# Key norms in an attention stage: from column sums, a root and spread products to products with ones, a logarithm and an exponential

## The chip, the cores and the metric

One core of one Trainium2 chip runs the whole program. The metric is the device time of one execution in microseconds (us), as the median of the runs; lower is better. TensorE multiplies matrices, VectorE, ScalarE and GpSimd work on elements, and each takes its instructions in the order in which they are written, with semaphores between them.

## The reference

The program is eight blocks on an activation x of 512 positions by 1024 channels: four mixers (a, b, c, a) and four sandwiched layers (e, f0, o, f1). Stage b is one of them, dilated window attention, with 8 heads of 128 channels and three patterns, each with its own query, key and value:

```python
def rms_norm(x, g):
    xf = x.astype(jnp.float32)
    y = xf * lax.rsqrt(jnp.mean(xf * xf, axis=-1, keepdims=True) + EPS)
    return (y * g.astype(jnp.float32)).astype(x.dtype)
...
    for g, (window, dilation) in enumerate(B_PATTERNS):
        q = apply_partial_rotary(rms_norm(qkv[:, :, 0, g], q_gain[g]), cos, sin)
        k = apply_partial_rotary(rms_norm(qkv[:, :, 1, g], k_gain[g]), cos, sin)
        o, lse = dilated_window_attention(q, k, qkv[:, :, 2, g], window // dilation, dilation)
        outs.append(o)
        lses.append(lse)
    wgt = jax.nn.softmax(jnp.stack(lses), axis=0)
    o = jnp.einsum('gbsh,gbshd->bshd', wgt, jnp.stack(outs))
    y = o.reshape(bsz, S, B_WIDTH).astype(h.dtype) * jax.nn.silu(z)
    return y @ w_out
```

Each query and each key row is divided by the root of its mean square over 128 channels. That division is what changes here.

## The kernel before

Weights come as units of 128x1024 by DMA into `raw`. ScalarE rounds a unit to the type that TensorE takes in one pass (`split_high`, L277, `w_high`), VectorE subtracts to get the rest (`split_low`, L284, `w_low`), three units ahead of TensorE. A product of a unit is 24 matmuls (`product`, L297 to L299): high by high, high by low, low by high.

Stage b works in two halves of four heads. A half begins with the values of its heads (L779 to L781), kept in `b_v`. Then comes a list of slots (j, u), written out for each engine in the same order, and `b_steps` says what a slot holds. Slot (j, u) projects tile u of head j: u = 0, 1, 2 are the keys of the three patterns, 3, 4, 5 the queries. The tile lies with channels in the partitions and the 512 positions in the row. One slot later the tile is squared, summed and turned by rotary. In slots 1 to 4 of head j the softmax of one block of 128 queries of head j-1 is done; in slots 2 to 5 the block of the slot before is transposed; in 3, 4, 5 and the next 0 it is multiplied by the values. Four slots with j = 4 project the gate z and finish the last head.

In a slot, TensorE does: the product of the tile; four column sums of the last tile's squares against a column of ones (L839, 128x1 each); value products (L853); transposes (L859 to L862); the score products, one of 128x512 (L871) and two small (L875); and in slots 4, 5 and the next 0 the spread: 1/rms of a key tile is made into a 128x512 bank by four products with the unit matrix (L885), for VectorE to multiply the keys with (L1068). The two small score products wait for ScalarE's copy of the last two transposes (L929), since they share a bank.

ScalarE in a slot: L277 for a unit ahead; the square of the new tile out of the bank (L909, in two buffers by turns); the tile with its gain (L915, "gained"); in two slots of a head a root of 12 columns (L923); copies of the transposes (L929, L931); Exp of the softmax (L934). A table load stands ahead of the root or Exp when the function set changes.

VectorE in a slot: L284; rotary on 32 rows (L1008, L1010, L1011, L1014); mean square plus epsilon (L1019) and reciprocals (L1028, L1031) in two slots of a head; scores with their scale and mask into `b_p` (L1048), maximum (L1052), its negative (L1054); behind Exp the reciprocal and the scaling of the row (L1060, L1062); the key multiply (L1068). GpSimd does nothing in stage b but the sums of squares for the next norm at its end (L325).

Of the kernel before, what the change touches and what calls it, by code (L numbers as in the profile page):

```python
# [27 lines left out]
F32 = mybir.dt.float32  # L28
# [3 lines left out]
P = 128  # L32
# [125 lines left out]
def build(nc, stream, x_in, params_in, const_in, tables_in, ssm_in, x_out):  # L158
# [10 lines left out]
    with ctx:  # L169
# [65 lines left out]
        b_root_done, b_rk_done, b_rq_done = sem("b_root_done"), sem("b_rk_done"), sem("b_rq_done")  # L235
        b_spread, b_k_done = sem("b_spread"), sem("b_k_done")
# [475 lines left out]
        b_sq = (sq, ssq)  # L712
        b_tanh = ssq[:]
# [3 lines left out]
        b_root, b_rk, b_rq = b_col[:, 0:24], b_col[:, 24:36], b_col[:, 36:60]  # L717
# [4 lines left out]
        def b_tile(j, n):  # L722
            return b_qk[:, (j % 2) * (B_TILES - 1) + n if n < B_TILES - 1 else 2 * B_TILES - 2]

# [34 lines left out]
        def b_tensor(pe, t, first, o, y_base, r, last=False, following=None):  # L759
# [39 lines left out]
            for i in range(2):  # L799
# [6 lines left out]
                for j, u in B_SLOTS:  # L806
                    unit = b_unit(first, i, j, u)
                    tile, s, tr, pv, kn = b_steps(j, u)
                    if unit is not None:
                        n = B_TILES * j + u  # L810
                        if n < 2:
                            pe.wait_ge(b_v_copied, lin(9 + n, i, 12))
                        elif j < BH or u < 2:
                            pe.wait_ge(b_gained, lin(n - 1, i, 24))
                        elif u == 2:
                            pe.wait_ge(b_args, lin(2 * BH, i, 2 * BH))
                        else:
                            pe.wait_ge(b_k_done, lin(3 * BH, i, 3 * BH))
                        product(pe, unit, ps[:, u if j == BH else n % 2], h_high, h_low)
                    elif i == 0:  # L820
                        values(1, 0, B_TAIL.index((j, u)))
                    else:
                        for k in (2 * B_TAIL.index((j, u)), 2 * B_TAIL.index((j, u)) + 1):
                            for m in range(4):
                                out_tile(m, k)
                    if (i, j, u) == (0, 0, 0):
                        norm_spread(pe, R_PRE["b"], 7).then_inc(b_r_spread, 1)
                    if tile is not None:
# [3 lines left out]
                        if tile[1] == 0 and n > 0:  # L832
                            pe.wait_ge(b_root_done, lin(2 * tile[0], i, 2 * BH))
                        if tile[1] == 3:
                            pe.wait_ge(b_root_done, lin(2 * tile[0] + 1, i, 2 * BH))
# [42 lines left out]
                    if kn is not None:  # L878
                        j0, g = kn
                        if 3 * j0 + g > 0:  # L880
                            pe.wait_ge(b_k_done, lin(3 * j0 + g, i, 12))
                        pe.wait_ge(b_rk_done, lin(j0 + 1, i, BH))
# [10 lines left out]
        def b_scalar(act, first, o, y_base, r, last=False, following=None):  # L893
            norm_root(act, R_PRE["b"])
            for i in range(2):
                for n in range(len(B_TAIL) * i, 4 * B_PATTERNS):
                    split_high(act, Unit(first + n + AHEAD, i, B_HALF))
                for j, u in B_SLOTS:
# [21 lines left out]
                    if tile is not None and tile[1] in (2, 5):  # L920
                        c = 12 * (tile[1] // 3)
                        act.wait_ge(b_args, lin(2 * tile[0] + tile[1] // 3 + 1, i, 2 * BH))
                        nc.scalar.activation(b_root[:, c:c + 12], b_root[:, c:c + 12], ACT.Sqrt).then_inc(b_root_done, 1)  # L923
# [8 lines left out]
                    if s is not None:  # L932
                        act.wait_ge(b_soft, b_soft_at(i, s[0], s[1], 5))
                        nc.scalar.activation(b_p, b_p, ACT.Exp, bias=b_neg, accum_out=b_sum).then_inc(b_exp, 1)  # L934
                    if j == BH and u < BH:
                        act.wait_ge(b_z_taken, BH * i + u + 1)
                        if u == 0:
                            act.wait_ge(b_ss, 6 * BH * (i + 1))
                        else:
# [7 lines left out]
            for m in range(KD):  # L947
# [4 lines left out]
                high_of(act, following, m)  # L952

        def b_vector(dve, first, o, y_base, r, last=False, following=None):
# [5 lines left out]
            for i in range(2):  # L960
# [25 lines left out]
                def take_z(m):  # L986
                    if i == 0:
                        dve.wait_ge(b_r_kept, 1)
                    if m == 0:
                        dve.wait_ge(b_ss, lin(6 * BH - 1, i, 6 * BH))  # L990
# [3 lines left out]
                for j, u in B_SLOTS:  # L994
# [21 lines left out]
                    if tile is not None and tile[1] in (2, 5):  # L1016
                        c = 12 * (tile[1] // 3)
                        dve.wait_ge(b_ss, lin(6 * tile[0] + tile[1] + 1, i, 24))
                        nc.vector.scalar_tensor_tensor(  # L1019
                            out=b_root[:, c:c + 12].rearrange("p (g b) -> p g b", b=NBLK),  # L1020
                            in0=ps[:, 2, c:c + 12].rearrange("p (g b) -> p g b", b=NBLK), scalar=1.0 / P,
                            in1=norm_eps.unsqueeze(1).to_broadcast([P, B_PATTERNS, NBLK]), op0=ALU.mult,
                            op1=ALU.add).then_inc(b_args, 1)
                    if tile is not None and tile[1] == 2:
                        dve.wait_ge(b_root_done, lin(2 * tile[0] + 1, i, 2 * BH))
                        if tile[0] > 0:
                            dve.wait_ge(b_spread, lin(3 * tile[0], i, 12))
                        nc.vector.reciprocal(b_rk, b_root[:, 0:12]).then_inc(b_rk_done, 1)  # L1028
                    if tile is not None and tile[1] == 5:
                        dve.wait_ge(b_root_done, lin(2 * tile[0] + 2, i, 2 * BH))  # L1030
                        nc.vector.reciprocal(b_rq[:, 12:24], b_root[:, 12:24]).then_inc(b_rq_done, 1)  # L1031
                        dve.wait_ge(b_rq_done, lin(2 * tile[0] + 1, i, 2 * BH))
                        if tile[0] > 0:
                            dve.wait_ge(b_soft, b_soft_at(i, tile[0] - 1, 3, 3))
                        nc.vector.tensor_scalar(b_rq[:, 0:12], b_rq[:, 12:24], P ** -0.5, None,
                                                op0=ALU.mult).then_inc(b_rq_done, 1)
                    if s is not None:
# [3 lines left out]
                        dve.wait_ge(b_rq_done, lin(2 * j0 + 2, i, 2 * BH))  # L1041
# [21 lines left out]
                    if kn is not None:  # L1063
                        j0, g = kn
                        n = 3 * j0 + g
                        dve.wait_ge(b_spread, lin(n + 1, i, 12))
                        dve.wait_ge(b_qk_done, lin(6 * j0 + g + 1, i, 24))
                        nc.vector.tensor_tensor(b_tile(j0, g), b_tile(j0, g), ps[:, 3], ALU.mult).then_inc(b_k_done, 1)  # L1068
# [1938 lines left out]
        def _(pool):  # L3007
            norm_gather(pool, 0)
            for n, name in enumerate(names):
                last = n == len(names) - 1  # L3010
                r = R_POST.get(name, None if last else R_PRE[name] + 1)
                if name == "e":
# [245 lines left out]
```

## Time and profile before

| | us |
|---|---|
| median of 3 runs | 3021.32 (3019.75 to 3021.74) |
| profiled execution, own time | 3030.46 |
| its span | 3028.7 |
| TensorE busy in it | 2924.4 (97%) |
| VectorE busy | 1714.8 (57%) |
| ScalarE busy | 1061.6 (35%) |
| GpSimd busy | 213.1 (7%) |

Busy times are sums over the span; matmuls are pipelined, so the duration of one is longer than the distance from its start to the next one's start. Where the text adds up time on an engine, it uses distances between starts. The slots of stage b lie between 463 and 1036 us of the span.

### The profile page before, as it was taken

What the parts mean: (1) busy time and instruction counts of PE and PEld (TensorE: products, weight loads), DVE (VectorE), ACT (ScalarE), POOL (GpSimd) and SP (SyncE); (2) the same over time, 40 slices, a digit from 0 to 9 for tenths busy, and PEclk for the clock granted to TensorE, in tenths of its full rate; (3) what the DMA queues carried; (4) which work ended last, traced back from release to release, by engine and by line L of the source; (5) the groups of instructions that cost most, each with busy time, mean ns of one, the idle gap of its engine ahead of it and who ended that gap; (6) DMA issues with size and microseconds to landing.
All of it is one profiled execution on the core that took longest, in us unless ns stands there. A gap on an engine that the chain in (4) does not pass through costs nothing.

```text
span 3028.7 us, 38678 instructions
## 1 busy us (share of the span) xinstructions
PE 2924.4 (97%) x14206; PEld 2413.4 (80%) x14206; DVE 1714.8 (57%) x2639; ACT 1061.6 (35%) x1601; POOL 213.1 (7%) x256
## 2 busy tenths in 40 slices
PE   7999999999999999999999999989999988999998
PEld 6888888888888778878888876588888875788887
DVE  5555535765576666654455576646444576464445
ACT  4332323443344332224332323434232345442222
POOL 1000000000000000001000000015502110110001
PEclk9999999999999999999999999989999999999999
DMA  4322232122221233332232331013333310223332
GB/s 146 97 96 85 92 104 77 56 63 77 78 62 56 63 105 95 95 97 90 90 97 83 97 102 45 29 55 106 92 95 96 99 63 16 62 85 96 96 97 90
DMA packets 70400, 252.14 MB, mean 83 GB/s; under 512 B 7808, under 2 KB 9856, under 8 KB 69632
## 3 DMA queue, kind: packets, MB, share of 16 engines
q1 hardware_dynamic: 68112, 241.89, 25.9%
q10 hardware_dynamic: 2016, 7.96, 0.7%
q8 instruction: 87, 1.43, 0.2%
q0 software_dynamic: 144, 0.52, 0.0%
q14 instruction: 41, 0.34, 0.0%
HBM read 248.25 MB, written 2.10 MB: 83 GB/s over the span
## 4 chain that ended last, share of the span: by engine, by line
PE 84%; DVE 8%; ACT 4%; issue 3%; POOL 1%; DMA 0%; DVEq 0%; ACTq 0%; POOLq 0%
PE ps L297 17%; PE ps L299 17%; PE ps L298 17%; PE ps L568 2%; PE ps L569 2%; PE ps L570 2%; ACT w_high L277 2%; DVE w_low L284 2%; PE ps L779 1%; PE ps L780 1%; PE ps L781 1%; PE ps L1803 1%; PE ps L853 1%; PE ps L591 1%; PE ps L839 1%
## 5 line engine op out<-in xcount | busy, mean ns | idle before, releaser
L284 DVE TENSOR_TENSOR w_low<-raw,w_high 128x1024 fp32r<-128x1024 f32 x456 | 565.8, 1246 | 420.8 <-ACT w_high L277 413.7
L297 PE MATMUL ps<-h_high,w_high 128*128 128x512 f32 x1872 | 737.8, 394 | 6.4 <-DVE arena L1464 3.0
L299 PE MATMUL ps<-h_high,w_low 128*128 128x512 f32 x1872 | 729.9, 390 | 0.0
L298 PE MATMUL ps<-h_low,w_high 128*128 128x512 f32 x1872 | 729.4, 390 | 0.0
L277 ACT ACTIVATE w_high<-raw 128x1024 fp32r<-128x1024 f32 x456 | 477.9, 1051 | 450.9 <-PE ps L299 204.0
L297 PEld LDWEIGHTS ps<-h_high,w_high 128*128 128x128 f32 x1872 | 352.3, 188 | 78.3 <-DVE arena L1464 3.4
L299 PEld LDWEIGHTS ps<-h_high,w_low 128*128 128x128 f32 x1872 | 351.8, 188 | 73.9
L298 PEld LDWEIGHTS ps<-h_low,w_high 128*128 128x128 f32 x1872 | 352.3, 188 | 70.1
L297 PE MATMUL ps<-y_high,w_high 128*128 128x512 f32 x640 | 250.4, 391 | 0.6 <-DVE y_low L1938 0.3
L298 PE MATMUL ps<-y_low,w_high 128*128 128x512 f32 x640 | 249.1, 389 | 0.0
L299 PE MATMUL ps<-y_high,w_low 128*128 128x512 f32 x640 | 249.0, 389 | 0.0
L325 POOL TENSOR_TENSOR root<-root,ssq 128x512 f32<-128x512 f32 x24 | 32.9, 1372 | 1691.5 <-ACT ssq L313 1690.0
L297 PEld LDWEIGHTS ps<-y_high,w_high 128*128 128x128 f32 x640 | 120.1, 188 | 28.0 <-DVE y_low L686 2.0
L299 PEld LDWEIGHTS ps<-y_high,w_low 128*128 128x128 f32 x640 | 120.1, 188 | 25.0
L298 PEld LDWEIGHTS ps<-y_low,w_high 128*128 128x128 f32 x640 | 120.2, 188 | 24.5
L568 PE MATMUL ps<-w_high,h_high 128*128 128x512 f32 x256 | 102.6, 401 | 11.4 <-DVE w_low L284 11.4
L569 PE MATMUL ps<-w_low,h_high 128*128 128x512 f32 x256 | 101.8, 397 | 0.0
L570 PE MATMUL ps<-w_high,h_low 128*128 128x512 f32 x256 | 101.6, 397 | 0.0
L1556 ACT ACTIVATE y_high<-full 128x512 f32 (+1 forms) x44 | 27.8, 632 | 192.2 <-DVE full L1590 192.2
L779 PE MATMUL ps<-w_high,h_high 128*128 128x512 f32 x192 | 76.8, 400 | 3.2 <-DVE x L520 2.1
L780 PE MATMUL ps<-w_low,h_high 128*128 128x512 f32 x192 | 75.8, 395 | 0.0
L781 PE MATMUL ps<-w_high,h_low 128*128 128x512 f32 x192 | 75.7, 394 | 0.0
(443 smaller groups left out, 4526.0 us busy)
## 6 DMA issues: line engine op xcount, KB each, us to landing
raw<-stream SPq DMA_DIRECT2D x456, 512.0 KB, 3.6
table<-tables_in ACTq DMA_DIRECT2D x5, 1088.0 KB, 6.5
x<-x_in ACTq DMA_DIRECT2D x8, 256.0 KB, 8.3
x_out<-x SPq DMA_DIRECT2D x16, 128.0 KB, 1.7
const<-const_in SPq DMA_DIRECT2D x1, 673.0 KB, 7.9
arena<-ssm_in POOLq DMA_DIRECT2D x1, 512.0 KB, 5.8
params<-params_in ACTq DMA_DIRECT2D x1, 287.0 KB, 6.7
```

The costliest lines, as they stand in the source:

```text
L277: nc.scalar.activation(w_high[:, u.slot], raw[:, u.raw], ACT.Copy).then_inc(weights_high, 1)
L284: nc.vector.tensor_tensor(w_low[:, u.slot], raw[:, u.raw], w_high[:, u.slot].bitcast(F32), ALU.subtract).then_inc(weights_low, 1)
L297: nc.tensor.matmul(bank, wh, high[:, k], start=k == 0, stop=False)
L298: nc.tensor.matmul(bank, wh, low[:, k], start=False, stop=False)
L299: mm = nc.tensor.matmul(bank, wl, high[:, k], start=False, stop=k == tiles - 1)
L325: nc.gpsimd.tensor_tensor(root[:], root[:], (sq, ssq)[m % 2][:], ALU.add).then_inc(norm_gathered, 1)
L568: nc.tensor.matmul(bank, hh, wh, start=k == 0, stop=False)
L569: nc.tensor.matmul(bank, hh, wl, start=False, stop=False)
L570: mm = nc.tensor.matmul(bank, hl, wh, start=False, stop=k == KD - 1)
L779: nc.tensor.matmul(bank, hh, wh, start=k == 0, stop=False)
L780: nc.tensor.matmul(bank, hh, wl, start=False, stop=False)
L781: mm = nc.tensor.matmul(bank, hl, wh, start=False, stop=k == KD - 1)
```

## The change

Only stage b changes, and in it the norms. The keys: ScalarE squares a key tile twice, once as it is and once rounded to the one-pass type (`b_halves(n)[0]`, in free rows of `y_high`); GpSimd subtracts to get the rest (new function `b_gpsimd`, into `y_low`); TensorE multiplies both parts with a 128x128 matrix of ones, which sums over the channels and leaves the sum in all 128 partitions. VectorE scales it and adds epsilon, which was spread by TensorE once at the start (`b_eps`). In slot 3, behind the softmax's Exp, ScalarE takes the logarithm of the three key tiles and then exp of minus one half of it. The key multiply reads that from SBUF. The spread products are gone. The queries keep their column sums; their 1/rms is now exp of minus half the logarithm too, for 12 columns in slot 0 of the next head. There is one buffer of squares in place of two.

```diff
-                        pe.wait_ge(b_gained, lin(n + 1, i, 24))
-                        for b in range(NBLK):
-                            c = 4 * tile[1] + b
-                            mm = nc.tensor.matmul(ps[:, 2, c:c + 1], b_blk(b_sq[n % 2], b), ones[:, 0:1],
-                                                  start=True, stop=True)
+                        if tile[1] < 3:
...
+                            pe.wait_ge(b_low, lin(3 * tile[0] + tile[1] + 1, i, 3 * BH))
+                            sq_high, sq_low = b_halves(n)
+                            nc.tensor.matmul(ps[:, 3], b_ones, sq_high, start=True, stop=False)
+                            mm = nc.tensor.matmul(ps[:, 3], b_ones, sq_low, start=False, stop=True)
...
-                    if kn is not None:
...
-                        for b in range(NBLK):
-                            col = b_rk[:, 4 * g + b:4 * g + b + 1].to_broadcast([P, P])
-                            mm = nc.tensor.matmul(b_blk(ps[:, 3], b), col, ident, start=True, stop=True)
-                        mm.then_inc(b_spread, 1)
...
-                            if n >= 2:
-                                act.wait_ge(b_ss, lin(n - 1, i, 24))
-                            nc.scalar.activation(b_sq[n % 2][:], ps[:, n % 2], ACT.Square)
+                            if n >= 1:
+                                act.wait_ge(b_ss, lin(n, i, 24))
+                            nc.scalar.activation(b_sq, ps[:, n % 2], ACT.Square)
+                            if u < 3:
+                                nc.scalar.activation(b_halves(n)[0], ps[:, n % 2], ACT.Square)
...
-                        nc.scalar.activation(b_root[:, c:c + 12], b_root[:, c:c + 12], ACT.Sqrt).then_inc(b_root_done, 1)
+                    if tile is not None and tile[1] == 5:
+                        act.wait_ge(b_args, lin(4 * tile[0] + 4, i, 4 * BH))
+                        nc.scalar.activation(b_root, b_root, ACT.Ln, scale=float(P)).then_inc(b_logs_done, 1)
...
+                        nc.scalar.activation(b_rq, b_root, ACT.Exp, scale=-0.5).then_inc(b_rq_done, 1)
...
+                    if tile is not None and tile[1] == 2:
+                        act.wait_ge(b_args, lin(4 * tile[0] + 3, i, 4 * BH))
+                        for g in range(B_PATTERNS):
+                            mm = nc.scalar.activation(b_log[g], b_log[g], ACT.Ln)
+                        mm.then_inc(b_logs_done, 1)
+                        act.wait_ge(b_logs_done, lin(2 * tile[0] + 1, i, 2 * BH))
+                        for g in range(B_PATTERNS):
+                            nc.scalar.activation(b_log[g], b_log[g], ACT.Exp, scale=-0.5).then_inc(b_rk_done, 1)
...
+        def b_gpsimd(pool):
+
+            for i in range(2):
+                for j in range(BH):
+                    for g in range(B_PATTERNS):
+                        n = B_TILES * j + g
+                        sq_high, sq_low = b_halves(n)
+                        pool.wait_ge(b_gained, lin(n + 1, i, 24))
+                        nc.gpsimd.tensor_tensor(sq_low, b_sq, sq_high.bitcast(F32), ALU.subtract).then_inc(b_low, 1)
...
+                        nc.vector.scalar_tensor_tensor(out=b_log[tile[1]], in0=ps[:, 3], scalar=1.0 / P, in1=b_eps,
+                                                       op0=ALU.mult, op1=ALU.add).then_inc(b_args, 1)
...
-                        nc.vector.tensor_tensor(b_tile(j0, g), b_tile(j0, g), ps[:, 3], ALU.mult).then_inc(b_k_done, 1)
+                        nc.vector.tensor_tensor(b_tile(j0, g), b_tile(j0, g), b_log[g], ALU.mult).then_inc(b_k_done, 1)
```

The line numbers shift by the change: square L909 to L918 (the second one L920), gained L915 to L926, copies L929 and L931 to L946 and L948, Exp L934 to L951, Ln L955 and Exp L959 for keys, L936 and L940 for queries.

ScalarE in slot 3 of a head, before. It begins with the weight rounding of the slot and ends with that of slot 4.

```order
L277 ACTIVATE w_high<-raw 128x1024
L909 ACTIVATE ssq<-ps 128x512
L915 ACTIVATE arena<-ps,params 128x512
L923 ACT_TABLE_LOAD
L923 ACTIVATE arena<-arena 128x12
L929 ACTIVATE work<-ps 128x256
L931 ACTIVATE work<-ps 128x512
L934 ACT_TABLE_LOAD
L934 ACTIVATE arena<-arena 128x768
L277 ACTIVATE w_high<-raw 128x1024
```

The same place after, from the copies of the transposes on; `full` and `const` hold the three tiles of logarithms.

```order
L946 ACTIVATE work<-ps 128x256
L948 ACTIVATE work<-ps 128x512
L951 ACTIVATE arena<-arena 128x768
L955 ACT_TABLE_LOAD
L955 ACTIVATE full<-full 128x512 x2
L955 ACTIVATE const<-const 128x512
L959 ACT_TABLE_LOAD
L959 ACTIVATE full<-full 128x512 x2
L959 ACTIVATE const<-const 128x512
L277 ACTIVATE w_high<-raw 128x1024
```

The root ahead of the copies has gone, and two table loads and six activations of 128x512 stand between the softmax's Exp and the next rounding.

ScalarE in slot 0 of the next head after the change, where the queries' 12 columns are done.

```order
L277 ACTIVATE w_high<-raw 128x1024
L918 ACTIVATE sq<-ps 128x512
L920 ACTIVATE y_high<-ps 128x512
L926 ACTIVATE arena<-ps,params 128x512
L936 ACT_TABLE_LOAD
L936 ACTIVATE arena<-arena 128x12
L940 ACT_TABLE_LOAD
L940 ACTIVATE arena<-arena 128x12
L277 ACTIVATE w_high<-raw 128x1024
```

Before, one table load and one root stood where the four rows L936 to L940 stand now, and the square was one.

TensorE in slot 2 of a head, behind the product, before and then after.

```order
L839 MATMUL ps<-const,ssq 128x1 x4
L859 MATMUL ps<-const,arena 128x128
L860 MATMUL ps<-const,arena 128x128
L862 MATMUL ps<-const,arena 128x128 x4
L871 MATMUL ps<-arena 128x512
L875 MATMUL ps<-arena 128x128 x2
```

```order
L849 MATMUL ps<-y_high 128x512
L850 MATMUL ps<-y_low,y_high 128x512
L877 MATMUL ps<-const,arena 128x128
L878 MATMUL ps<-const,arena 128x128
L880 MATMUL ps<-const,arena 128x128 x4
L889 MATMUL ps<-arena 128x512
L893 MATMUL ps<-arena 128x128 x2
```

Four products of one column have become two of 512; the rest stands as it stood.

## Rows read from the trace of the kernel before

**Rows 1.** Busy time, share and instructions, from the page.

```profile
PE 2924.4 (97%) x14206; PEld 2413.4 (80%) x14206; DVE 1714.8 (57%) x2639; ACT 1061.6 (35%) x1601; POOL 213.1 (7%) x256
```

**Rows 2.** Waits from 440 to 1110 us: who for whom, us in total, times, longest.

```profile
PEld ps L875 <- ACT work L929: 11.4, 24, 1.3
```

**Rows 3.** Groups on TensorE, 440 to 1110 us: busy us, mean ns.

```profile
L885 PE MATMUL ps<-const,arena 128*128 128x128 f32 x192 | 25.8, 278 | 0.0
```

**Rows 4.** Timeline of ScalarE: start us, duration us, slot 0 of heads 1 to 3.

```profile
508.47 0.60 ACT L909 ACTIVATE sq<-ps 128x512 f32<-128x512 f32 x1 [5.13 <-PE ps L299]
...
561.48 0.60 ACT L909 ACTIVATE sq<-ps 128x512 f32<-128x512 f32 x1 [4.84 <-PE ps L299]
...
615.84 0.60 ACT L909 ACTIVATE sq<-ps 128x512 f32<-128x512 f32 x1 [4.84 <-PE ps L299]
```

**Rows 5.** Timeline of TensorE's weight loads, slots 4 and 5 of head 2.

```profile
595.59 1.09 PEld L839 LDWEIGHTS ps<-const,ssq 128*128 128x128 f32 x8
596.61 1.42 PEld L853 LDWEIGHTS ps<-work,arena 128*128 128x128 f32 x12
...
599.14 0.19 PEld L875 LDWEIGHTS ps<-arena 128*128 128x128 f32 x1 [0.24 <-ACT work L929]
...
599.91 0.97 PEld L885 LDWEIGHTS ps<-const,arena 128*128 128x128 f32 x8
600.80 0.19 PEld L297 LDWEIGHTS ps<-h_high,w_high 128*128 128x128 f32 x1
...
606.14 1.09 PEld L839 LDWEIGHTS ps<-const,sq 128*128 128x128 f32 x8
...
609.15 0.97 PEld L885 LDWEIGHTS ps<-const,arena 128*128 128x128 f32 x8
```

**Rows 6.** Timeline of VectorE, slots 2 to 5 of head 2.

```profile
576.86 1.23 DVE L284 TENSOR_TENSOR w_low<-raw,w_high 128x1024 fp32r<-128x1024 f32 x1 [0.23 <-ACT w_high L277]
...
578.76 0.68 DVE L1010 TENSOR_TENSOR root<-root,table 32x512 f32<-32x512 f32 x1
...
580.68 1.25 DVE L1048 SCALAR_TENSOR_TENSOR arena<-ps,arena,table 128x512 f32<-128x512 f32 x3
...
585.25 1.23 DVE L284 TENSOR_TENSOR w_low<-raw,w_high 128x1024 fp32r<-128x1024 f32 x1 [0.23 <-ACT w_high L277]
...
604.49 0.68 DVE L1068 TENSOR_TENSOR arena<-arena,ps 128x512 f32<-128x512 f32 x1
605.09 1.22 DVE L284 TENSOR_TENSOR w_low<-raw,w_high 128x1024 fp32r<-128x1024 f32 x1
```

**Rows 7.** ScalarE: timeline of head 2, then its group for Tanh.

```profile
562.68 1.28 ACT L923 ACT_TABLE_LOAD   x1
563.97 0.21 ACT L923 ACTIVATE arena<-arena 128x12 f32<-128x12 f32 x1
...
583.14 0.94 ACT L934 ACTIVATE arena<-arena 128x768 f32<-128x768 f32 x1 [3.31 <-DVE arena L1054]
...
584.08 1.05 ACT L277 ACTIVATE w_high<-raw 128x1024 fp32r<-128x1024 f32 x1
...
606.57 0.60 ACT L909 ACTIVATE ssq<-ps 128x512 f32<-128x512 f32 x1 [1.89 <-PE ps L299]
607.06 0.68 ACT L915 ACTIVATE arena<-ps,params 128x512 f32<-128x512 f32 x1
609.08 0.38 ACT L929 ACTIVATE work<-ps 128x256 f32<-128x256 f32 x1 [1.34 <-PE ps L860]
...
L941 ACT ACTIVATE ssq<-sq 128x512 f32<-128x512 f32 x4 | 2.5, 633 | 5.6 <-DVE sq L992 5.1 <-DVE root L972 0.5
```

**Rows 8.** GpSimd and VectorE at the end of stage b, timelines.

```profile
1043.22 1.29 POOL L325 TENSOR_TENSOR root<-root,ssq 128x512 f32<-128x512 f32 x1 [657.11 <-ACT ssq L313]
1047.70 2.52 POOL L325 TENSOR_TENSOR root<-root,sq 128x512 f32<-128x512 f32 x1 [3.19 <-ACT sq L313]
...
1043.35 2.25 DVE L284 TENSOR_TENSOR w_low<-raw,w_high 128x1024 fp32r<-128x1024 f32 x1
```

More of the change, by code:

```diff
@@ L827, in b_tensor @@
                         norm_spread(pe, R_PRE["b"], 7).then_inc(b_r_spread, 1)
+                        pe.wait_ge(b_v_copied, 12)
+                        for b in range(NBLK):
+                            mm = nc.tensor.matmul(b_blk(ps[:, 3], b), norm_eps[:, b:b + 1].to_broadcast([P, P]), ident,
+                                                  start=True, stop=True)
+                        mm.then_inc(b_r_spread, 1)
                     if tile is not None:
@@ L831, in b_tensor @@
                             pe.wait_ge(b_v_copied, lin(12, i, 12))
[L832 to L835, printed above, removed]
-                        pe.wait_ge(b_gained, lin(n + 1, i, 24))
-                        for b in range(NBLK):
-                            c = 4 * tile[1] + b
-                            mm = nc.tensor.matmul(ps[:, 2, c:c + 1], b_blk(b_sq[n % 2], b), ones[:, 0:1],
-                                                  start=True, stop=True)
+                            if i == 0:
+                                pe.wait_ge(b_r_kept, 2)
+                        if tile[1] < 3:
+                            if tile[1] > 0:
+                                pe.wait_ge(b_args, lin(4 * tile[0] + tile[1], i, 4 * BH))
+                            elif n > 0:
+                                pe.wait_ge(b_args, lin(4 * tile[0] - 1, i, 4 * BH))
+                            pe.wait_ge(b_low, lin(3 * tile[0] + tile[1] + 1, i, 3 * BH))
+                            sq_high, sq_low = b_halves(n)
+                            nc.tensor.matmul(ps[:, 3], b_ones, sq_high, start=True, stop=False)
+                            mm = nc.tensor.matmul(ps[:, 3], b_ones, sq_low, start=False, stop=True)
+                        else:
+                            if tile[1] == 3 and n > 3:
+                                pe.wait_ge(b_args, lin(4 * tile[0], i, 4 * BH))
+                            pe.wait_ge(b_gained, lin(n + 1, i, 24))
+                            for b in range(NBLK):
+                                c = 4 * tile[1] + b
+                                mm = nc.tensor.matmul(ps[:, 2, c:c + 1], b_blk(b_sq, b), ones[:, 0:1],
+                                                      start=True, stop=True)
                         mm.then_inc(b_ss, 1)
@@ L1015, in b_vector @@
                                                 ALU.add).then_inc(b_qk_done, 1)
-                    if tile is not None and tile[1] in (2, 5):
-                        c = 12 * (tile[1] // 3)
+                    if tile is not None and tile[1] < 3:
+                        if (i, tile) == (0, (0, 0)):
+                            dve.wait_ge(b_r_kept, 2)
                         dve.wait_ge(b_ss, lin(6 * tile[0] + tile[1] + 1, i, 24))
+                        nc.vector.scalar_tensor_tensor(out=b_log[tile[1]], in0=ps[:, 3], scalar=1.0 / P, in1=b_eps,
+                                                       op0=ALU.mult, op1=ALU.add).then_inc(b_args, 1)
@@ L1019, in b_vector @@
+                    if tile is not None and tile[1] == 5:
+                        dve.wait_ge(b_ss, lin(6 * tile[0] + 6, i, 24))
                         nc.vector.scalar_tensor_tensor(
-                            out=b_root[:, c:c + 12].rearrange("p (g b) -> p g b", b=NBLK),
-                            in0=ps[:, 2, c:c + 12].rearrange("p (g b) -> p g b", b=NBLK), scalar=1.0 / P,
+                            out=b_root.rearrange("p (g b) -> p g b", b=NBLK),
+                            in0=ps[:, 2, 12:24].rearrange("p (g b) -> p g b", b=NBLK), scalar=1.0 / P,
@@ L1029, in b_vector @@
[L1029 to L1036, printed above, removed]
```

47 lines of the change are left out of this document (21 added, 26 removed).

## The prediction

> **What bounds the kernel now.** I read the page first. TensorE is busy 97% of the span [rows 1], so what a change takes off TensorE is worth its time wherever nothing else steps in. The second view is the list of waits over stage b. What TensorE's weight loads waited for there is short: the largest, the two small score products waiting for ScalarE's copy of the first transposes, comes to 11.4 us in 24 waits over two halves [rows 2]. Stage b runs at TensorE's own pace.
>
> The third view is the timeline of one steady head. A head has six slots, and slot u runs the 24 matmuls of projection tile u, then small work on the tile and on the attention of the head before it. ScalarE's squares show the period: slot 0 of head 1, 2 and 3 at 508.47, 561.48 and 615.84, so 53.01 and 54.36 us a head [rows 4]. TensorE's pieces come from the starts of its weight loads [rows 5]: a projection tile 5.34 (600.80 to 606.14), four column sums 1.02 (595.59 to 596.61), four spread products 0.89 (599.91 to 600.80), the two small score products 0.77 (599.14 to 599.91), and sums, value products and transposes together 3.01 (606.14 to 609.15).
>
> The fourth reading is of what runs beside it. In a slot with a softmax, VectorE splits a weight (L284), turns the tile by rotary (L1008 to L1014), scales scores and takes their maximum; ScalarE runs Exp and only then rounds the next weight (L277); and VectorE's next split needs that one. This is a loop through two engines. It took 8.39 us from the split at 576.86 to the one at 585.25 [rows 6], with no wait for TensorE in it (the scores at 580.68 show none), while a slot of TensorE lasts 54.36 / 6 = 9.06 on average. So TensorE bounds the head, with 0.7 us a slot to spare where a softmax runs. That margin decides this case.
>
> **The change, part by part.**
>
> TensorE loses the 24 groups of spread products of a key tile (192 records for 96 matmuls of two passes each [rows 3]): 24 x 0.89 = 21.4 us. Of the 48 groups of column sums, the 24 of key tiles become two 128x512 products of the split kind. A projection tile issues 24 of that kind in 5.34, so 0.22 each and 0.45 for two, in place of 1.02: 24 x 0.57 = 13.7 us. One spread of the epsilon row is added, 0.9 us. If TensorE stayed the bound, the change would be worth 21.4 + 13.7 - 0.9 = 34.2 us.
>
> VectorE gets a 128x512 scale-and-add out of PSUM in slots 1, 2 and 3. Its nearest row is L1068, 0.60 from start to next start (604.49 to 605.09) [rows 6]. It stands between the rotary and the softmax, inside the loop: 8.39 + 0.60 = 8.99 us a slot. Two reciprocals and a small multiply of 12 columns go, which gives nothing here, for slot 5 and slot 0 have room. The key multiply keeps its size; it reads SBUF now, not PSUM.
>
> ScalarE squares each key tile a second time (0.5 from start to start, 606.57 to 607.06), and there is one buffer of squares for two, so the square of a tile waits for TensorE's sum of the tile before, which stands behind the tile's own product. Then come Ln and Exp on three 128x512 tiles in slot 3, behind the softmax's Exp and ahead of slot 4's weight rounding. The order of the program shows one table load ahead of the Ln and one ahead of the Exp. Neither function on 128x512 in SBUF is in the trace; nearest is Tanh on the same shape and source, 633 ns, less 0.1 of overlap where one follows another. The block: 0.1 to drain, load 1.28, Ln 0.53 + 0.53 + 0.65, load 1.28, Exp 3 x 0.53, together 5.96 us [rows 7]. From below it can't cost less than two loads and six times 0.50, 5.6; from above, six times 0.63 and the loads, 6.4 plus the drain. Nothing hides it: VectorE's split in slot 4 waits for the rounding behind it, and so do the rotary, the softmax, and ScalarE's own squaring and copy of slot 4, for which TensorE's small scores wait. In slot 0 the twelve query columns cost load, Ln, load, Exp, 1.28 + 0.21 + 1.28 + 0.21 = 2.98, where one load and a root stood.
>
> GpSimd gets 24 subtractions of 128x512. TensorE needs one only after the next 5.34 us tile, so its 1.3 us are hidden. Their effect on VectorE isn't. At the end of stage b GpSimd's add ran from 1043.22 for 1.29 us, and the weight split that VectorE began at 1043.35 took 2.25 us, against 1.23 in every row of [rows 6]; another of GpSimd's adds, at 1047.70, took 2.52 [rows 8]. The rows say: one of the two stands still until the other is done. In slot 2 the subtraction can start when ScalarE has gained the tile, 1.6 us after the start of VectorE's split (0.5 + 0.5 + 0.65 behind the rounding), and lasts to 2.9; VectorE's first rotary multiply starts 1.9 behind the split (576.86 to 578.76). It waits 1.0 us, inside the loop. Bounds: 0 if they miss each other, 1.3 for each of three subtractions.
>
> The Trainium skill has this rule (SBUF — State Buffer, Who interferes with whom): a VectorE instruction with two SBUF inputs and a GpSimd instruction that reads SBUF exclude each other for a whole instruction. The trace agrees, 2.25 against 1.23. It speaks against this change: by the rule and by the rows alike about 1 us a head is added, and without it none.
>
> **The chain of a head after the change.** I add it up from the end of the product of slot 0. Sum of query tile 5 on TensorE and the signal, 1.02 + 0.2 (an estimate; the signal behind a whole tile took 0.43, 606.14 to 606.57) = 1.2. ScalarE squares twice and gains, 0.5 + 0.5 + 0.7, to 2.9. The query block 2.98, to 5.9. Rounding to split 1.17 (584.08 to 585.25), to 7.1. Slots 1 and 2 at 8.99 each, to 25.1. Slot 3 at 8.99 + 5.96, to 40.0. Now from slot 4's rounding, 1.17 earlier at 38.9: 1.05 rounding, 0.5 square, 0.65 gain, 0.38 copy (L929), to 41.4; small scores 0.77, product of slot 5 5.34, to 47.6; 3.01, to 50.6; product of slot 0, 5.34, to **55.9 us**. TensorE alone would need 54.36 - 3 x 0.57 - 3 x 0.89 = 50.0. The bound changes hands: before 54.36 by TensorE, after 55.9 by the loop, and 56.9 with the wait for GpSimd.
>
> **Sum for a half.** Head 0 has no softmax beside it and stays with TensorE: three pairs at -0.57, two spreads at -0.89, -3.5. Head 1: 56.9 - 53.0 = +3.9. Heads 2 and 3: 2 x (56.9 - 54.4) = +5.0. The slot behind the last head loses its spread, -0.9. Together +4.5; two halves +9.0; epsilon row +0.9; so +10 us. The profiled execution has a span of 3028.7, and 3030.46 as a whole, 9 above the median of the runs, 3021.32; the difference lies outside this sum, so I add to the median: **3031 us**. What the measurement can tell from no change is 0.2%, 6 us.
>
> **Rivals.**
> *TensorE stays the bound.* The ScalarE block would have to be hidden. For it: slots 5 and 0 have no softmax, and so room on VectorE. Against: 55.9 against 50.0 leaves 5.9 us a head to find, and the block stands in a slot with a softmax. It would give 3021 - 34 = 2987.
> *The loop binds, but costs less.* If the 5.96 us block shrank by the 2.6 us of its two loads, and the query block likewise, the chain would be 55.9 - 5.2 = 50.7, and with GpSimd's 1.0 51.7: head 1 -1.3, heads 2 and 3 -2.6 each, with -4.4 as before -10.9 a half, 3021 - 21 = 3000. This ends on the other side; it decides from 1.7 us less than I add in each of the six heads with a softmax beside them (10 / 6). The Trainium skill (ScalarE: Activation LUTs, Table sets: the hidden batching unit) has Ln and Exp in one set, one load for both. By that page the sum would be about this; the program's order has two loads, and no run here shows which set each takes.
> *GpSimd misses VectorE.* 55.9 a head: -3.5 + 2.9 + 3.0 - 0.9 = +1.5 a half, with the epsilon row +4, so 3025, within 0.2%.
> *Worse contact with GpSimd.* All three subtractions of a head hit the loop, 3.9 us for 1.0 in six heads: +17 more, 3048.
>
> **How the numbers follow.** Forecast 0.55. Worse contact 0.10. GpSimd misses 0.15. Cheaper loop 0.13. TensorE stays the bound 0.07. The last two are the 0.20 for faster by over 0.2%; same takes the third and a small part of the forecast's lower edge, 0.18; slower has 0.62. The forecast's own range, with the block at 5.6 to 6.5 and the contact at 0.5 to 1.3, is 3025 to 3040. The range reaches to 3050 above, which takes in the worse contact, and to 3006 below; the two faster cases stay out, 0.20 between them.
>
> **What would show each step.** TensorE's busy time falls by tens of us, but it has new idle time ahead of the small scores (L893), released by ScalarE's copy, in slot 4 by some 2 to 5 us. VectorE waits for the rounding L277 about 6 us in slot 4. The starts of ScalarE's squares in slot 0 of heads 2 and 3 are 56 to 58 apart. Rotary multiplies, 0.68 each, stretch towards 1.7 beside GpSimd's rows. The block from first load to last Exp takes 5.9. I am wrong if Ln comes without a load of its own, if a head keeps to 50 us, or if the rotary rows don't stretch.

## The result, and the profile of the changed kernel

The changed kernel takes 3048.73 us (median of 5, 3043.07 to 3050.97) against 3021.74 (5 runs, 3019.75 to 3030.01) beside it: ratio 1.0084, 95% interval 1.0071 to 1.0096. It is slower by 27 us; the forecast said 10. The sign and most of the mechanism held. The time lies inside the stated range, but outside the forecast's own part of it (3025 to 3040): the room up to 3050 was left for a worse contact with GpSimd, which isn't what happened.

The first line of the page of the changed kernel, to be held against [rows 1]:

```profile
PE 2911.5 (95%) x13878; PEld 2391.8 (78%) x13878; DVE 1730.7 (57%) x2631; ACT 1103.6 (36%) x1680; POOL 247.2 (8%) x280
```

TensorE has less to do and the span is longer, so somewhere it waits. To find where, I measure stage b by itself: VectorE sums the column norms at its start and again at the start of the stage behind it (L396). Two timeline rows of VectorE after the change:

```profile
400.49 0.17 DVE L396 TENSOR_REDUCE norm_col<-ps 128x4 f32<-128x8 f32 x1 [8.00 <-PE ps L345]
...
1092.65 0.17 DVE L396 TENSOR_REDUCE norm_col<-ps 128x4 f32<-128x8 f32 x1 [1.97 <-PE ps L345]
```

The stage lasts 692.16 us. The same two rows of the kernel before start at 400.55 and 1072.05, 671.50 us. The 20.7 us between them are the whole of the 20.5 between the two profiled spans (3028.7 and 3049.2); outside the stage both traces take 2357 us. Engine busy times of this stretch, from the view by windows (columns: stretch, length, busy of PE, PEld, DVE, ACT, POOL, granted clock, DMA):

```profile
400.49:1092.65 692.16, 647.95 (x3153) 533.42 (x3154) 430.58 (x692) 307.73 (x471) 42.94 (x30) 0.96 0.22 69
```

Before, TensorE was busy 660.46 of 671.50 at a granted 0.99. Its idle time rose from 11 to 44 us, and its mean clock fell. The waits of stage b name the place (who for whom, us in total, times, longest):

```profile
DVE w_low L284 <- ACT w_high L277: 142.1, 64, 6.7
...
PEld ps L893 <- ACT work L946: 43.0, 24, 5.8
PE ps L893 <- ACT work L946: 28.4, 10, 5.0
```

[rows 2] had 11.4 us in the same 24 waits, longest 1.3. Now head 2 on ScalarE, with slots 0, 3 and 4 and the square of the next head's slot 0 (start us, duration us, what ended the idle time before):

```profile
565.83 0.60 ACT L918 ACTIVATE sq<-ps 128x512 f32<-128x512 f32 x1 [4.79 <-PE ps L857]
...
567.52 1.28 ACT L936 ACT_TABLE_LOAD   x1
568.81 0.21 ACT L936 ACTIVATE arena<-arena 128x12 f32<-128x12 f32 x1
569.04 1.28 ACT L940 ACT_TABLE_LOAD   x1
570.33 0.21 ACT L940 ACTIVATE arena<-arena 128x12 f32<-128x12 f32 x1
570.45 1.04 ACT L277 ACTIVATE w_high<-raw 128x1024 fp32r<-128x1024 f32 x1
...
598.31 1.28 ACT L955 ACT_TABLE_LOAD   x1
599.60 1.15 ACT L955 ACTIVATE full<-full 128x512 f32<-128x512 f32 x2
600.66 0.61 ACT L955 ACTIVATE const<-const 128x512 f32<-128x512 f32 x1
601.29 1.28 ACT L959 ACT_TABLE_LOAD   x1
602.59 1.15 ACT L959 ACTIVATE full<-full 128x512 f32<-128x512 f32 x2
603.64 0.61 ACT L959 ACTIVATE const<-const 128x512 f32<-128x512 f32 x1
604.16 1.04 ACT L277 ACTIVATE w_high<-raw 128x1024 fp32r<-128x1024 f32 x1
...
606.15 0.38 ACT L946 ACTIVATE work<-ps 128x256 f32<-128x256 f32 x1
...
624.35 0.60 ACT L918 ACTIVATE sq<-ps 128x512 f32<-128x512 f32 x1 [4.79 <-PE ps L857]
```

The key block runs from 598.31 to 604.16, 5.85 us (forecast 5.96). The weight rounding stands behind it, and behind that the copy (L946) for which TensorE waits. The squares of slot 0 are 58.52 us apart, where [rows 4] had 54.36. This head, from slot 0 of head 2 to slot 0 of head 3, is called the steady head below.

VectorE in the same head, with the two effects that the prediction named, and GpSimd's subtraction beside the first:

```profile
582.52 1.45 DVE L1043 TENSOR_TENSOR root<-root,table 32x512 f32<-32x512 f32 x1
...
605.33 1.23 DVE L284 TENSOR_TENSOR w_low<-raw,w_high 128x1024 fp32r<-128x1024 f32 x1 [6.19 <-ACT w_high L277]
```

```profile
582.15 1.28 POOL L985 TENSOR_TENSOR y_low<-sq,y_high 128x512 fp32r<-128x512 f32 x1 [5.47 <-ACT arena L926]
```

The rotary multiply takes 1.45 where its neighbours take 0.68, and ends 0.5 us behind GpSimd's subtraction (583.97 against 583.43). And TensorE, where the forecast stopped looking too early. Its timeline around slot 4:

```profile
606.58 1.22 PE L893 MATMUL ps<-arena 128*128 128x128 f32 x4 [4.99 <-ACT work L946]
607.46 0.77 PE L297 MATMUL ps<-h_high,w_high 128*128 128x512 f32 x1
608.03 0.63 PE L298 MATMUL ps<-h_low,w_high 128*128 128x512 f32 x1
...
611.45 0.41 PE L297 MATMUL ps<-h_high,w_high 128*128 128x512 f32 x1
...
614.92 0.95 PE L857 MATMUL ps<-const,sq 128*128 128x1 f32 x8
```

The same stretch by windows:

```profile
596.00:601.00 5.00, 5.00 (x36) 4.45 (x35) 1.94 (x5) 3.71 (x6) 0.00 (x0) 1.00 0.00 0
601.00:606.50 5.50, 0.60 (x2) 0.00 (x0) 1.17 (x3) 5.47 (x10) 0.00 (x0) 0.83 0.00 0
606.50:608.00 1.50, 1.42 (x5) 1.36 (x6) 1.47 (x4) 0.52 (x2) 0.00 (x0) 0.50 0.36 41
608.00:610.00 2.00, 2.00 (x6) 1.58 (x5) 1.97 (x4) 0.00 (x0) 0.00 (x0) 0.50 0.64 231
610.00:612.00 2.00, 2.00 (x7) 1.53 (x7) 1.51 (x4) 0.38 (x1) 0.00 (x0) 0.63 0.00 0
612.00:614.00 2.00, 2.00 (x10) 1.62 (x9) 1.29 (x3) 1.60 (x3) 0.00 (x0) 1.00 0.00 0
```

TensorE worked to about 601.6, then waited 5 us. It came back at a granted clock of 0.50, which is the 1.2 GHz level, and stood on it until past 611. A matmul of the product lasts 0.63 there and 0.39 to 0.41 later. Small scores and product together take 614.92 - 606.58 = 8.34 us, where the forecast had 0.77 + 5.34 = 6.11. The wait is paid a second time behind its end.

### The profile page after: what moved, and what is told of

Read it like the earlier page. It is cut to its first block, busy times and chain, and to the rows that moved or that the text cites. A ratio compares the mean times of both kernels' runs of the same rounds, so it can differ in the third digit from the quotient of the medians.

```text
span 3049.2 us, 38104 instructions
## 1 busy us (share of the span) xinstructions
PE 2911.5 (95%) x13878; PEld 2391.8 (78%) x13878; DVE 1730.7 (57%) x2631; ACT 1103.6 (36%) x1680; POOL 247.2 (8%) x280
## 4 chain that ended last, share of the span: by engine, by line
PE 81%; DVE 9%; ACT 6%; issue 3%; POOL 1%; DMA 0%; DVEq 0%; ACTq 0%; POOLq 0%
PE ps L297 17%; PE ps L298 17%; PE ps L299 17%; ACT w_high L277 2%; PE ps L568 2%; PE ps L570 2%; PE ps L569 2%; DVE w_low L284 2%; PE ps L784 1%; PE ps L786 1%; PE ps L785 1%; PE ps L1828 1%; PE ps L591 1%; PE ps L1409 1%; PE ps L1184 1%
## 5 line engine op out<-in xcount | busy, mean ns | idle before, releaser
L277 ACT ACTIVATE w_high<-raw 128x1024 fp32r<-128x1024 f32 x456 | 477.7, 1051 | 453.1 <-PE ps L299 204.5
L569 PE MATMUL ps<-w_low,h_high 128*128 128x512 f32 x256 | 101.7, 397 | 0.0
L570 PE MATMUL ps<-w_high,h_low 128*128 128x512 f32 x256 | 101.6, 397 | 0.0
L951 ACT ACTIVATE arena<-arena 128x768 f32<-128x768 f32 x32 | 30.0, 938 | 147.7 <-DVE arena L1079 147.7
L985 POOL TENSOR_TENSOR y_low<-sq,y_high 128x512 fp32r<-128x512 f32 x24 | 34.3, 1428 | 539.3 <-ACT arena L926 539.3
```

The source lines that it names most:

```text
L277: nc.scalar.activation(w_high[:, u.slot], raw[:, u.raw], ACT.Copy).then_inc(weights_high, 1)
L569: nc.tensor.matmul(bank, hh, wl, start=False, stop=False)
L570: mm = nc.tensor.matmul(bank, hl, wh, start=False, stop=k == KD - 1)
L985: nc.gpsimd.tensor_tensor(sq_low, b_sq, sq_high.bitcast(F32), ALU.subtract).then_inc(b_low, 1)
```

## The experiments

Every kernel was run beside the kernel before. Ratios go by medians. The whole program also differs between runs outside stage b, where no edit reaches: in the twelve traces the rest takes between 2344.7 and 2357.2 us. So what an edit does is read from the length of stage b in the profiled execution, by the same two rows of L396 each time: before 671.5, after 692.2.

**e1_move: the keys' Ln and Exp at another place.** Same work; the block moves from behind slot 3's softmax Exp to ahead of slot 4's, where ScalarE waits for VectorE's maximum.

```diff
-                    if s is not None:
-                        act.wait_ge(b_soft, b_soft_at(i, s[0], s[1], 5))
-                        nc.scalar.activation(b_p, b_p, ACT.Exp, bias=b_neg, accum_out=b_sum).then_inc(b_exp, 1)
-                    if tile is not None and tile[1] == 2:
+                    if tile is not None and tile[1] == 3:
                         act.wait_ge(b_args, lin(4 * tile[0] + 3, i, 4 * BH))
...
                             nc.scalar.activation(b_log[g], b_log[g], ACT.Exp, scale=-0.5).then_inc(b_rk_done, 1)
+                    if s is not None:
+                        act.wait_ge(b_soft, b_soft_at(i, s[0], s[1], 5))
+                        nc.scalar.activation(b_p, b_p, ACT.Exp, bias=b_neg, accum_out=b_sum).then_inc(b_exp, 1)
```

> The change, with only the keys' block of Ln and Exp (two table loads, six activations) moved on ScalarE: from behind the softmax's Exp of slot 3 to slot 4, behind the copies of the transposes and ahead of the softmax's Exp, where ScalarE now idles 4.6 us waiting for VectorE. Theory A (the block costs what it does because it stands ahead of slot 4's weight rounding, and TensorE's clock falls behind the wait that this makes): the block hides in that idle time up to 1.4 us, a steady head goes from 58.5 to about 52 us, TensorE waits nowhere for 5 us and its clock stays up; 6 heads x 6.5 = 39 us less than the changed kernel, about 3010. Theory B (what costs is the added work itself and GpSimd against VectorE): the same work is done, so the time stays within 6 us of 3049.

Measured: 3005.97 (3003.70 to 3012.52) against 3022.75, ratio 0.9949 [0.9932, 0.9966]; stage b 654.5, which is 37.7 less than the changed kernel. The steady head takes 50.93 (about 52 was expected). ScalarE's timeline, slot 4 of the same head:

```profile
596.11 0.38 ACT L946 ACTIVATE work<-ps 128x256 f32<-128x256 f32 x1
596.49 0.60 ACT L948 ACTIVATE work<-ps 128x512 f32<-128x512 f32 x1
597.10 1.28 ACT L952 ACT_TABLE_LOAD   x1
...
602.96 0.92 ACT L959 ACTIVATE arena<-arena 128x768 f32<-128x768 f32 x1
```

The copy is out before the block begins, and the softmax's Exp starts right behind it. What TensorE's loads wait for it, over both halves:

```profile
PEld ps L893 <- ACT work L946: 11.8, 24, 1.1
```

It is nearly back at the 11.4 of [rows 2]. The place of the block is the cause of the loss, and of more than the loss: the change itself, placed so, is a gain.

**e2_noln: no Ln for the keys.** The wait and the counts go with it.

```diff
                         for g in range(B_PATTERNS):
-                            mm = nc.scalar.activation(b_log[g], b_log[g], ACT.Ln)
-                        mm.then_inc(b_logs_done, 1)
-                        act.wait_ge(b_logs_done, lin(2 * tile[0] + 1, i, 2 * BH))
-                        for g in range(B_PATTERNS):
                             nc.scalar.activation(b_log[g], b_log[g], ACT.Exp, scale=-0.5).then_inc(b_rk_done, 1)
```

> The change with the keys' three Ln left out, so that Exp works on the mean squares themselves; with them go both table loads of slot 3, since Exp is loaded already. The result is not the reference's: keys are scaled wrongly. Theory A: the block shrinks from 5.9 to 1.6 us, TensorE's wait of 5 us in slot 4 to about 1; 4.3 us a head in six heads, 26 us, and up to 11 us of TensorE's clock on top: 3012 to 3023. Theory B: only the load and activation time of an engine that is 36% busy goes, 0 to 5 us, 3044 to 3049.

Measured: 3001.92, ratio 0.9935 [0.9918, 0.9953]; stage b 652.6, 39.6 less. The first Exp now starts right behind the softmax's, with no load, so the block shrank from 5.85 to the 1.56 us between 588.46 and 590.02. That is 4.29 us less in each of six heads, 26. TensorE's longest wait for the copy is 1.4 us now and its granted clock around slot 4 (586 to 600 us) is 1.00, so the 12 us that e4_warm below puts on the low clock go with them, 38 in all by this sum. The time itself is below the 3012 to 3023 expected, 46.8 less than the changed kernel: part of that lies outside stage b. This kernel and e1_move reach nearly the same time by different roads: the key block costs nothing once it is short or out of the way.

**e3_memset: GpSimd writes zeros.** It reads nothing any more.

```diff
-                        nc.gpsimd.tensor_tensor(sq_low, b_sq, sq_high.bitcast(F32), ALU.subtract).then_inc(b_low, 1)
+                        nc.gpsimd.memset(sq_low.bitcast(F32), 0.0).then_inc(b_low, 1)
```

> The change with GpSimd's subtraction replaced by a memset of the same 128x512 buffer to zero, so that GpSimd reads nothing; waits and order are kept. The low part of the squares is left out, so key norms are less exact. Theory A with the port as a small term: the rotary multiply of slot 2 is 0.7 to 1.0 us shorter in six heads and one or two more contacts go at the first softmax head, 5 to 8 us less, 3041 to 3044. If GpSimd against VectorE is the main cost: 17 us or more less, below 3032. If a memset holds VectorE up as a subtraction does: no change.

Measured: 3034.98, ratio 1.0044 [1.0030, 1.0057]; stage b 685.2, 7.0 less. The stage meets the expected 5 to 8; the time, 14 below the changed kernel's, misses the 3041 to 3044, with the rest outside stage b. The rotary groups of VectorE over the stage (busy us, mean ns | idle before), of the changed kernel and then of this one:

```profile
L1043 DVE TENSOR_TENSOR root<-root,table 32x512 f32<-32x512 f32 x48 | 37.1, 774 | 1.6
L1044 DVE TENSOR_TENSOR arena<-arena,table 32x512 f32<-32x512 f32 x48 | 34.5, 718 | 0.0
```

```profile
L1043 DVE TENSOR_TENSOR root<-root,table 32x512 f32<-32x512 f32 x48 | 32.6, 679 | 1.7
L1044 DVE TENSOR_TENSOR arena<-arena,table 32x512 f32<-32x512 f32 x48 | 32.3, 672 | 0.0
```

The contact exists. In the changed kernel it is in slot 2 of every head from 1 on, 0.7 to 0.8 us each, and in slot 1 of head 1 as well, 1.1 us:

```profile
515.28 1.76 DVE L1044 TENSOR_TENSOR arena<-arena,table 32x512 f32<-32x512 f32 x1
```

Together that is close to what the forecast said, 1.0 in six heads. The Trainium skill (SBUF — State Buffer, Who interferes with whom) restricts the conflict to a GpSimd instruction that reads SBUF, not one that only writes it; 679 against 774 ns agrees.

**e4_warm: TensorE kept busy in the wait.** 120 products are added whose result nobody reads; nothing is taken out.

```diff
                         nc.tensor.matmul(ps[:, 4], b_blk(b_tile(j0, 3), b), b_tile(j0, 0), start=True, stop=True)
+                        if j < BH and u == 4:
+                            pe.wait_ge(b_args, lin(4 * j + 3, i, 4 * BH))
+                            for _ in range(20):
+                                nc.tensor.matmul(ps[:, 3], b_ones, h_high[:, 0], start=True, stop=True)
```

> The change with 20 useless products of 128x512 put on TensorE in slot 4 of each head of 1 to 3, between the large score product and the two small ones, into the bank of the key sums: 4.4 us of work in the place where TensorE waits 5 us for ScalarE's copy. 120 products more in all. Theory C (the clock: behind that wait the product of slot 5 took 7.2 us in place of 5.3 at half the granted clock): the clock stays up, the product takes 5.3, and the kernel gets faster by 6 x 1.9 = 11 us, to about 3038, with more work. Rival (the slow product has another cause, or the wait is all there is): no change or slower, 3049 to 3055.

Measured: 3028.56 (3026.56 to 3039.66), ratio 1.0021 [1.0009, 1.0033]; stage b 680.2, 12.0 less. TensorE's timeline, slot 4 of the same head, and its windows:

```profile
602.94 0.71 PE L897 MATMUL ps<-arena 128*128 128x128 f32 x4 [0.46 <-ACT work L950]
603.41 0.48 PE L297 MATMUL ps<-h_high,w_high 128*128 128x512 f32 x1
603.72 0.40 PE L298 MATMUL ps<-h_low,w_high 128*128 128x512 f32 x1
...
608.95 0.95 PE L857 MATMUL ps<-const,sq 128*128 128x1 f32 x8
```

```profile
600.00:604.00 4.00, 3.54 (x18) 2.68 (x18) 2.28 (x4) 3.38 (x7) 0.00 (x0) 1.00 0.00 0
604.00:610.00 6.00, 6.00 (x33) 5.13 (x32) 4.77 (x11) 1.98 (x3) 0.00 (x0) 1.00 0.32 90
```

Small scores and product now take 6.01, at a granted 1.00, and ScalarE's block takes its 5.85 as before (594.66 to 600.51). The steady head falls from 58.52 to 56.21. So 12.0 us of stage b (11 expected) were the price of the low clock, shown and not argued. The median fell by 20, more than the 11 expected; the other 8 lie outside stage b.

**e0_after: the changed kernel again,** beside the next three.

> The changed kernel again, unaltered, beside the three that follow and the kernel before on one chip. Same program, so 3043 to 3051 and a ratio to before of 1.007 to 1.010; its stage b, from the last norm sum ahead of it to the first behind it, 20.7 us longer than before's 671.5. If the earlier kernels' gain over it came partly from another chip, it lies lower here.

Measured: 3045.63, ratio 1.0075 [1.0058, 1.0092]; stage b 692.3. It stands as the base of the next kernels; its stage b moved by 0.1, its median by 3.

**e5_two: two buffers of squares.** The epsilon row moves out of the second one's place.

```diff
-        b_sq, b_eps, b_tanh = sq[:], ssq[:], con("chunk", 0, T)
+        b_sq, b_eps, b_tanh = (sq[:], ssq[:]), y_low[:, 7].bitcast(F32), con("chunk", 0, T)
...
-                            if n >= 1:
-                                act.wait_ge(b_ss, lin(n, i, 24))
-                            nc.scalar.activation(b_sq, ps[:, n % 2], ACT.Square)
+                            if n >= 2:
+                                act.wait_ge(b_ss, lin(n - 1, i, 24))
+                            nc.scalar.activation(b_sq[n % 2], ps[:, n % 2], ACT.Square)
```

> The change with two buffers of squares again, by turns, as in the kernel before (the epsilon row moves to a free row of y_low, rounded to the one-pass type). Theory A says that the single buffer delays ScalarE's square by the sum of the tile before, 0.5 to 1.0 us, and that this is on the chain of a head only in slot 0: 0.7 us in six heads, 4 us, so 3 to 5 us less than the changed kernel. Rival (the single buffer is the main cost, since it couples ScalarE to TensorE in every slot): 15 us or more less.

Measured: 3040.80, ratio 1.0055 [1.0039, 1.0071]; stage b 688.9, 3.3 less, as expected. The single buffer is not the main cost.

**e6_hoist: e1_move, and slot 1's rounding ahead of the queries' block.**

```diff
-                    if b_split_unit(first, i, j, u) is not None:
+                    if b_split_unit(first, i, j, u) is not None and not (j >= 1 and u == 1):
                         split_high(act, b_split_unit(first, i, j, u) + AHEAD)
...
+                    if j >= 1 and j <= BH and u == 0:
+                        split_high(act, b_split_unit(first, i, j, 1) + AHEAD)
                     if tile is not None and tile[1] == 5:
```

> The kernel with the keys' block moved to slot 4, and the same thought applied to the queries' block: in slot 0 ScalarE rounds slot 1's weight ahead of it, so that VectorE's split and rotary run while the two loads, Ln and Exp do. VectorE waits 3 to 4 us for that rounding in slot 1 of each of heads 1 to 4. Theory A: a steady head goes from 50.9 to 50.3 and the first softmax head by 2 us, 3 to 6 us less than 3006: 3000 to 3003. Rival (TensorE is the bound of a steady head by now): no change, 3004 to 3008.

Measured: 3002.95, ratio 0.9932 [0.9916, 0.9948]; stage b 648.4, 6.2 less than e1_move. The steady head keeps its 50.9, where 50.3 was expected: with the key block out of the way it was nearly TensorE's own already. The gain is in head 1, the first with a softmax beside it, which goes from 55.65 to 52.73 in the first half and from 54.80 to 51.58 in the second, by the squares of slot 0.

**e7_all: e5_two and e6_hoist together,** and **e7b_again,** the same kernel run again.

> The last one with two buffers of squares as well. Theory A: TensorE's own work is then nearly all there is, 50.0 us a head; 2 to 4 us less than with the hoist alone, 2996 to 3001. Rival: no change against the hoist alone.

> The kernel with the keys' block in slot 4, slot 1's rounding ahead of the queries' block and two buffers of squares once more, for a narrower interval and to share a chip with the next. Same program: 2989 to 2999, ratio to before 0.988 to 0.992.

Measured: 2990.90, ratio 0.9905 [0.9886, 0.9924], and 2991.41, ratio 0.9897 [0.9880, 0.9913]; stage b 642.3 and 642.2. It beats both kernels. The buffer is worth 6.0 us of stage b here, more than its 3.3 alone, and more than the 2 to 4 expected. By windows and waits:

```profile
399.64:1041.85 642.21, 628.91 (x3153) 521.82 (x3154) 434.08 (x693) 306.58 (x471) 43.09 (x30) 0.99 0.25 75
```

```profile
PEld ps L893 <- ACT work L948: 11.5, 24, 1.0
...
PEld ps L877 <- DVE arena L1089: 3.4, 2, 1.7
```

TensorE is at 98% of the stage again, as before the change, with 31.6 us less to do.

**e8_memset: e7_all with zeros from GpSimd,** as in e3_memset.

> The same kernel with GpSimd's subtraction replaced by a memset (the low part of the squares is left out). In the changed kernel this took 7.0 us off stage b. Theory A: contact with GpSimd only costs where VectorE and ScalarE's loop is the bound; TensorE is that by now in a steady head (50.4 us against its own 50.0), so the memset brings 0 to 2 us. Rival: the contact costs wherever it is, 5 to 8 us less.

Measured: 2986.85, ratio 0.9880 [0.9863, 0.9896]; stage b 639.0, 3.2 less than e7b_again, between the two expectations. The steady head takes 50.37 in both: there the contact is hidden behind TensorE. The head that gains is head 1, 50.73 to 49.04 in both halves by the squares of slot 0. The waits of TensorE's loads ahead of L877, 3.4 us in e7b_again, are gone too.

## Why the prediction was right, and where its size was not

**The bound changes hands: right.** The loop through VectorE and ScalarE sets the head, TensorE waits ahead of L893 in slot 4, VectorE waits 6.19 for L277 (forecast about 6), and e1_move, which alters nothing but the place of the block, takes 37.7 us off stage b. The loop itself is as summed: in head 2 VectorE's splits of slots 1 to 4 start 8.99, 9.76 and 14.95 apart (571.63, 580.62, 590.38, 605.33), for 8.99, 9.99 with the contact, and 14.95.

**The blocks: right.** 5.85 for 5.96; in slot 0, 567.52 to 570.45, 2.93 for 2.98. Ln and Exp each had a load of its own. The Trainium skill (ScalarE: Activation LUTs, Table sets: the hidden batching unit) counts one load for the two, which was the rival at 3000. Over both halves the trace shows the Ln and Exp of keys and of queries with eight loads each, 32 of 1283 ns. Here the measurement decides against the page.

**GpSimd's contact: right in sum.** 1.0 us in six heads forecast, 7.0 in all measured by e3_memset, with two contacts in head 1 and one each in heads 2 and 3. The worse contact, 3048, was a rival whose number the result meets, but its mechanism isn't the reason: it priced the contact at 23 us. That the result falls inside the stated range is luck, since only this rival had moved the upper end from 3040 to 3050.

**What failed is one term of the chain: "small scores 0.77, product of slot 5 5.34".** Both durations were read from rows where TensorE had not waited. Behind a wait of 5 us they took 8.34 together instead of 6.11, because the granted clock was 0.50. e4_warm gives 2.3 of it back in the steady head and 12.0 in stage b, 2.0 for each of the six heads. Without the low clock the steady head would be the 56.21 of e4_warm, 0.7 under the forecast 56.9. With it head 2 takes 4.2 us more than before in the first half and 4.0 in the second, and not 2.5; head 3 takes 3.6 and 3.8 more by the starts of TensorE's products (617.70 to 675.97 after, 610.04 to 664.75 before); and head 1 takes 5.9 and 6.7 more, not 3.9. Head 1 has the second contact besides: in e4_warm, with the clock up, it is still 4.7 longer than before. I had forecast the idle time, 2 to 5 us of it, but treated TensorE as an engine that comes out of a wait as it went in.

**Head 0: right, but the squares hide it.** From square to square of slot 0, head 0 lost 1.4 and 2.3 us, not 3.5. It has to be read on TensorE. These are the starts of the products of slot 0 of heads 0 and 1, before and then after:

```profile
462.73 0.19 PEld L297 LDWEIGHTS ps<-h_high,w_high 128*128 128x128 f32 x1 [1.27 <-DVE arena L967]
...
502.70 0.19 PEld L297 LDWEIGHTS ps<-h_high,w_high 128*128 128x128 f32 x1
```

```profile
462.67 0.19 PEld L297 LDWEIGHTS ps<-h_high,w_high 128*128 128x128 f32 x1 [1.27 <-DVE arena L1000]
...
500.34 0.19 PEld L297 LDWEIGHTS ps<-h_high,w_high 128*128 128x128 f32 x1
```

39.97 has become 37.67, 2.3 less, with the epsilon row's 0.9 in it, which the sum counted by itself; in the second half, without that row, 39.03 has become 35.85. So head 0 lost 3.2 in both halves. The other 0.85 is the square of head 1's slot 0, which waits for the sum of tile 5 since there is one buffer: it starts 6.62 behind its product's start, where it was 5.77. The key block costs nothing here: ScalarE's square behind it comes late (8.00 behind the one before, where it was 6.36), but TensorE's product starts don't. Per half the stage has +10.4 and +10.3; the forecast had +4.5 in each, and the epsilon row's 0.9 once.

**What the change takes off TensorE: right.** 34.2 us were forecast if TensorE stayed the bound. e7_all reaches 29.2 of it in stage b, with all the work of the change in it. So the gain was not an illusion; in the changed kernel the order of ScalarE's work, and for a smaller part the single buffer, took it, and 20.7 us more.

**What stays open.** The medians differ by 27 and stage b by 20.7; the profiled spans by 20.5. The rest, some 6 us in the medians, isn't in the traces' stage b, as part of what the experiments gained isn't (e4_warm: 20 in the median, 12.0 in stage b). Nothing was changed in the other stages, and yet the part of the program behind stage b takes from 1948.4 to 1956.7 us in the twelve traces: 1956.7 and 1956.6 in those of the kernel before and the changed one, 1948.9 in e4_warm's. A difference of 6 to 8 us in a median can be no more than this; what sets it is open, and no experiment was aimed at it. Nor did I separate why the second buffer of squares is worth more once the blocks are out of the way.

## What to carry to other kernels

A block of side work goes on an engine's queue where that engine waits anyway, not ahead of the operation that another engine's loop needs: with the same block of 5.85 us the change made this kernel 27 us slower in one place and, with the change's gain then free, 17 us faster than the kernel before in the other. When a chain is summed, the price of a wait of TensorE includes the matmuls behind it: take their durations from rows that follow a wait of that length, or bound them from above by the slower level. And a change that lightens the bound is worth its time only as far as the next loop reaches, so sum that loop first, and then look which of its parts need not be in it.

## What the runs showed of the hardware

TensorE waited 4.99 us, came back at 606.58 at a granted clock of 0.50, and was at 1.00 again only past 611; 20 products without use in the wait kept it at 1.00 and made the kernel faster. The low clock can also set in behind the wait: in head 1 TensorE waited 3.77 us, to 548.75, its first 128x512 matmuls took 0.39 to 0.47 at a granted 1.00, and from 550.36 they took 0.63 (the granted clock is 0.57 on average from 550.20 to 554.00). A wait of VectorE or ScalarE of like length left no such mark: the split after 6.19 us took its 1.23, the square after 4.79 us its 0.60. Ln on 128x512 in SBUF takes 623 ns and Exp 621. GpSimd's write of zeros does not touch VectorE's rotary multiplies (none over 0.68), its subtraction holds them up by 0.7 to 1.1 us.
